# Split weights of the units with 256 moving columns, placed 64 bytes further on in their slots

## The reference, cut to what matters

```python
z = h @ w_in                              # odd: 1024 -> 3104 columns
proj = h @ w_in[l]                        # mix: 1024 -> 3584 columns
q = (h @ w_q).reshape(B, S, MEM_HEADS, MEM_HEAD_DIM)
k, v = jnp.split(m @ w_kv, 2, axis=-1)    # m: the 256 memory tokens
x = x + 0.5 * swiglu_2(rmsnorm(x, ffn2_norm[l]), ffn2_w_gu[l], ffn2_w_down[l])
```

## Time and profile before

| | us |
|---|---|
| three runs, median | 2511.64 |
| three runs, lowest and highest | 2505.56, 2512.35 |
| the profiled execution, its own time | 2508.56 |
| its span, first instruction to last | 2506.6 |
| PE busy | 2434.8 (97% of the span) |
| weight loads busy | 2029.8 (81%) |
| DVE, ACT, POOL busy | 1238.3, 892.2, 74.3 |
| granted TensorE clock, mean | 0.984 of full speed |

### The profile page before, as it was taken

How to read it: one execution, slowest core, us unless ns; L and a number is a source line. 1 busy time by engine, 2 the same in 40 slices (tenths; PEclk the granted TensorE clock), 3 DMA queues, 4 the chain that set the end, 5 groups by cost and what they waited for, 6 DMA issues and landing times.

```text
span 2506.6 us, 30267 instructions
## 1 busy us (share of the span) xinstructions
PE 2434.8 (97%) x12270; PEld 2029.8 (81%) x12270; DVE 1238.3 (49%) x1476; ACT 892.2 (36%) x1202; POOL 74.3 (3%) x81
## 2 busy tenths in 40 slices
PE   7989999999999999999999999999989999999998
PEld 6658888888899778888888888789968877888886
DVE  6687543357746543332354442446676544444423
ACT  3353323313345333332333331335355444333311
POOL 0210000000012000000000000000000000000000
PEclk9999999998999999999999999999999999999999
DMA  8215522463232222222222222221111212222221
GB/s 333 77 69 234 184 104 97 151 247 139 93 123 88 78 69 99 100 100 96 89 84 100 100 94 100 87 101 68 68 51 68 84 68 84 84 100 98 87 101 66
DMA packets 40405, 267.34 MB, mean 107 GB/s; under 512 B 4378, under 2 KB 5658, under 8 KB 9218
## 3 DMA queue, kind: packets, MB, share of 16 engines
q1 hardware_dynamic: 31248, 219.87, 24.4%
q0 software_dynamic: 5696, 40.37, 4.2%
q10 hardware_dynamic: 3378, 5.91, 0.8%
HBM read 263.90 MB, written 2.24 MB: 106 GB/s over the span
## 4 chain that ended last, share of the span: by engine, by line
PE 88%; DVE 7%; ACT 3%; DMA 1%; issue 1%; SPq 0%; DVEq 0%; ACTq 0%
PE bank L227 26%; PE bank L228 25%; PE bank L229 25%; PE bank L2223 1%; DVE w_lo L214 1%; ACT w_hi L210 1%; DMA work<-stream 1%; PE bank L2138 1%; PE bank L330 1%; PE bank L1864 1%; PE bank L2200 1%; DVE work L457 1%; PE bank L2212 1%; DVE work L441 1%; PE bank L1860 1%
## 5 line engine op out<-in xcount | busy, mean ns | idle before, releaser
L227 PE MATMUL bank<-h_hi,w_hi 128*128 128x512 f32 x1800 | 711.6, 395 | 5.4 <-DVE w_lo L214 2.2
L228 PE MATMUL bank<-h_lo,w_hi 128*128 128x512 f32 x1800 | 704.0, 391 | 0.0
L229 PE MATMUL bank<-h_hi,w_lo 128*128 128x512 f32 x1800 | 703.8, 391 | 0.0
L214 DVE TENSOR_TENSOR w_lo<-raw,w_hi 128x2048 fp32r<-128x2048 f32 x192 | 439.9, 2291 | 478.9 <-ACT w_hi L210 478.9
L210 ACT ACTIVATE w_hi<-raw 128x2048 fp32r<-128x2048 f32 x192 | 366.3, 1908 | 414.0 <-PE bank L229 410.5
L227 PEld LDWEIGHTS bank<-h_hi,w_hi 128*128 128x128 f32 x1800 | 340.0, 189 | 82.6 <-issue 6.7
L229 PEld LDWEIGHTS bank<-h_hi,w_lo 128*128 128x128 f32 x1800 | 339.9, 189 | 71.8
L228 PEld LDWEIGHTS bank<-h_lo,w_hi 128*128 128x128 f32 x1800 | 340.1, 189 | 70.5 <-issue 1.4
L229 PE MATMUL bank<-g_hi,w_lo 128*128 (+1 forms) x704 | 273.9, 389 | 0.0
L227 PE MATMUL bank<-g_hi,w_hi 128*128 (+1 forms) x704 | 273.9, 389 | 0.0
L228 PE MATMUL bank<-g_lo,w_hi 128*128 (+1 forms) x704 | 273.9, 389 | 0.0
(11 more groups left out here) (321 smaller groups left out, 2799.7 us busy)
## 6 DMA issues: line engine op xcount, KB each, us to landing
raw<-stream SPq DMA_DIRECT2D x192, 1024.0 KB, 4.8
work<-stream POOLq DMA_DIRECT2D x19, 1024.0 KB, 7.0
h_plain<-stream POOLq DMA_DIRECT2D x16, 1024.0 KB, 5.4
work<-stream SPq DMA_DIRECT2D x13, 1024.0 KB, 12.3
work<-mlstm_rows ACTq DMA_DIRECT2D x8, 512.0 KB, 4.8
x<-xT SPq DMA_DIRECT2D x1, 2048.0 KB, 9.8
outT<-work SPq DMA_DIRECT2D x8, 256.0 KB, 2.2
work<-mlstm_rows ACTq DMA_DIRECT2D x8, 192.0 KB
```

The source lines that it names most:

```text
L214: nc.vector.tensor_tensor(w_lo[:, slot(m), :], raw[:, slot(m), :], w_hi[:, slot(m), :], ALU.subtract).then_inc(lo_split, 1)
L227: nc.tensor.matmul(out, stationary[0], moving[0], start=first, stop=False)
L228: nc.tensor.matmul(out, stationary[0], moving[1], start=False, stop=False)
L229: return nc.tensor.matmul(out, stationary[1], moving[0], start=False, stop=last)
```

## The change

Each of the two slots of `w_hi` and `w_lo` grows by 32 words (128 bytes). A set `beside` lists the 22 units with 256 moving columns, and a helper `words(m)` gives the place of unit m within its slot: from word 16 (64 bytes) for those, from word 0 for all others. Both splits write there, and all readers take it from there. No instruction is added, removed or moved on any engine, and `raw` stays as it was.

Addresses after: `w_hi` 82048 as before and its second slot 128 bytes further on than before; `w_lo` 98688, that is 256 bytes further on, its second slot 384; everything behind them 512 bytes further on (`work` 125824). All these steps are multiples of 128. So, counted modulo 128, only the weights of the 22 units move, by 64.

```diff
--- before.py
+++ after.py
@@ -113,8 +113,8 @@
         h_lo = place("h_lo", [P, KC, S], F32R)
         h_plain = place("h_plain", [P, 4, UNIT], offset=at[0] - 4 * UNIT * 4)
         raw = place("raw", [P, 2, UNIT])
-        w_hi = place("w_hi", [P, 2, UNIT], F32R)
-        w_lo = place("w_lo", [P, 2, UNIT], F32R)
+        w_hi = place("w_hi", [P, 2, UNIT + 32], F32R)
+        w_lo = place("w_lo", [P, 2, UNIT + 32], F32R)
 
         par = place("par", [P, N_PARAMS])
         tab = place("tab", [P, N_TABLES])
@@ -198,6 +198,15 @@
         def slot(m):
             return m % 2
 
+        beside = set()
+        for name, units in (("odd_in", range(5, 13)), ("mix_in", (4, 5, 6, 7, 12, 13)), ("mem_kv", range(7)), ("mem", (4,))):
+            beside.update(FIRST_UNIT[name] + u for u in units)
+
+        def words(m):
+
+            c = 16 if m in beside else 0
+            return slice(c, c + UNIT)
+
         def place_of(m):
 
             return ADA_UNITS + m
@@ -207,11 +216,11 @@
             act.wait_ge(landed[slot(m)], 16 * (m // 2 + 1) + 16 * i)
             if m >= 2:
                 act.wait_ge(unit_used, m - 1 + 2 * i)
-            nc.scalar.activation(w_hi[:, slot(m), :], raw[:, slot(m), :], ACT.Copy).then_inc(hi_split, 1)
+            nc.scalar.activation(w_hi[:, slot(m), words(m)], raw[:, slot(m), :], ACT.Copy).then_inc(hi_split, 1)
 
         def split_lo(dve, m, i=0):
             dve.wait_ge(hi_split, m + 1 + 2 * i)
-            nc.vector.tensor_tensor(w_lo[:, slot(m), :], raw[:, slot(m), :], w_hi[:, slot(m), :],
+            nc.vector.tensor_tensor(w_lo[:, slot(m), words(m)], raw[:, slot(m), :], w_hi[:, slot(m), words(m)],
                                     ALU.subtract).then_inc(lo_split, 1)
 
         def split_next_hi(act, m, i=0):
@@ -230,7 +239,7 @@
 
         def unit_cols(m):
 
-            return [w[:, slot(m), :].rearrange("p (k n) -> p k n", k=KC) for w in (w_hi, w_lo)]
+            return [w[:, slot(m), words(m)].rearrange("p (k n) -> p k n", k=KC) for w in (w_hi, w_lo)]
 
         def features(pe, m, block, out, wait_chunk=None, src=None, i=0):
 
@@ -834,7 +843,7 @@
 
                 def rows(d, i, first=False, end=False):
                     m = self.md + d
-                    wh, wl = (w[:, slot(m), :].rearrange("p (k n) -> p k n", k=2) for w in (w_hi, w_lo))
+                    wh, wl = (w[:, slot(m), words(m)].rearrange("p (k n) -> p k n", k=2) for w in (w_hi, w_lo))
                     pe.wait_ge(lo_split, m + 1 + 2 * i)
                     order = [(k, o) for k in range(2) for o in range(KC)]
                     early, late = 2 * slot(self.md), 2 * slot(self.md + 1)
```

## The result

The changed kernel is slower: 2526.25 us (median of 4 runs, 2524.55 to 2530.14) against 2510.54 for the kernel before beside it (2505.56 to 2512.35). The ratio is 1.0073, 95% interval 1.006 to 1.0086. The prediction, 2506.5 with a range up to 2520, is missed on the slow side. The profiled execution took 2525.41 us with a span of 2523.4; before, 2508.56 with 2506.6. So 16.8 us have to be found in the trace, at the same mean granted clock (0.984 in both).

A forecast was written before the change was run, and what follows sets the result against it. TensorE was taken as the bound, paced by intervals between matmul starts. From the profiled 2508.6 us, 2.6 us gained on 256-column matmuls, all else 0, gave 2506.0; allowing for run scatter it predicted 2506.5, range 2495 to 2520.

The forecast's parts named there:

- TensorE is the bound, and what a matmul gains or loses arrives at the end: Whole kernel: TensorE busy 97% of the span; a matmul's gain or loss where the changed units run arrives almost one to one.
- The addresses decide: Weight load beside matmul stream: their phase, and so addresses, sets the interval; 256 columns settle at a poor value, 120 ns.
- the restart rows: Profile rows after a break: eight 256-column intervals average 117.5 ns against 120 settled; ten 512-column ones 231 against 226.8.
- Rival A: Placement plays no part; the 13 ns are a fixed price of a float32r matmul with its load: 2508.6 us, chance 0.12.
- 256 columns at 118 ns, 2.6 us gained: The 22 changed units: 1300 settled intervals go from 120 to 118 ns, gaining 2.6 us.
- Rival B: 256-column matmuls: load and stream no longer meet, interval 111.6 to 115 ns, gain 7.5 to 12.9 us, chance 0.34.
- C: 256-column matmuls: load and stream meet more often, 4.2 to 13 ns each, 6.8 to 21 us lost, chance 0.15.
- Modulo 128 a shift by 64 is the same either way, so one answer serves all 1728.: The 22 units' 1728 matmuls: shifting load or stream by 64 bytes was taken to have one and the same effect.
- Splits at nothing: 22 of the 192 ACT and DVE splits, 64 bytes further on: covered by PE, taken as 0; 4.6 us if uncovered.
- A step of 256 does not matter then; one of 128 no row shows. I take 0.: Second slots 128 bytes further on, `w_lo` 256, `work` 512: effect of these moves on everything else taken as 0.
- Rival D: Second slots' 128 bytes matter for every other unit of all shapes: half of 5400 at 3 ns, 8 us, 2517, chance 0.04.
- The signs to look for: Trace checks: about 256 instructions in the 30 us 256-column run, 134 in the 512-column window, loads 0.19 us, splits unchanged.

## Why the prediction was wrong

- *TensorE is the bound, and what a matmul gains or loses arrives at the end.* Right: +16.2 us busy, +16.8 us of span.
- *The addresses decide.* Right, as the restart rows had suggested. Moving only the activations (ratio 1.0112) shows it without the change. Rival A falls. That load and stream collide is the reading that fits; no run shows the collision itself.
- *256 columns at 118 ns, 2.6 us gained.* The sign held; the size was half. In the changed kernel the long run settles at 117.8 in one slot and 113.3 in the other, and all gain 3.1 ns in the mean, 5.1 us. The kernel with the shift and 256 bytes of room has 117.8 in the long run, the value forecast. That it was hit is partly luck: it came from the average of restarted intervals, and the same argument would have given 118 for 192 bytes, which settled at 113.3. Rival B was right for some units and C for none.
- *"Modulo 128 a shift by 64 is the same either way, so one answer serves all 1728."* The runs do not bear this out: the period is 256 and the sign counts. With 64 bytes and a room of 256 the weights that move settle at 117.8, and the units of `mem_kv` with weights that stay run at 113.5 in their longest stretch, in the mean at 115.7 to 116.1.
- *Splits at nothing.* Right: 1908 and 2290 ns.
- *"A step of 256 does not matter then; one of 128 no row shows. I take 0."* This is the step that failed, and the forecast with it. The first half holds (the room of 256 bytes). The second gave the value 0 and the chance 0.04 to a term for which no bounds were taken, though it touched half of all units and so some 4000 of the 512-column matmuls, more than twice as many as the change names. Bounds from both sides by the nearest rows were worked out for 1728 matmuls and not for these. By the earlier trace rows the term would have had an upper bound of 4.2 to 13 ns each, 17 to 52 us for 4000; a range that ends at 2520 holds not even the lower.
- *Rival D's price, 3 ns on half of 5400, 8 us.* The mechanism was right, and both factors too small: 5.5 ns on 3981 matmuls (`g`, `o` and `mixed` streams count as well), 21.8 us. Less the 5.1 gained, plus 0.8 in the first slots, that is the loss. D's own text had the direction ("512 columns sit near their best phase"), and what stood against it was a step of 256 alone, which says nothing of 128.
- *The signs to look for.* The loads kept their 0.19 us. 133 in the 512-column window was named as D's, and came. The 256 instructions in the 256-column run came too, but stand for a mean of two paces. The odd pieces and the long run moved the same way. The interval was not to leave 115 to 125; the mean of 116.5 stays inside, the second slots of the long run with 113.3 do not.

The Trainium skill, "SBUF — State Buffer", section "SBUF: two separate sides", says that TensorE's two read ports are independent and never wait on anyone, and the prediction drew from it that nothing would change. The runs contradict that: with `h` alone moved by 128 bytes against the weights, a 512-column matmul takes 232.6 ns rather than 226.7. The gap of "TensorE: Matmul & The Clock Gate", section "Back-to-back issue gap", 109.2 ns for 256 columns by its formula, was reached in no settled unit; the lowest is 113.3. In the Trainium skill that formula stands for the isolated gap, not for a stream of loads and matmuls, so it was no measure of what 64 bytes could free.

**What stays open.** What the two reads collide on was not measured, only that the addresses and the previous state decide. Why one distance settles at 113.3 once and at 117.8 another time is open as well. The unit with both paces shows that it can change across a dip of the clock; what then selects the pace was not tried, and with one trace of each kernel it is not known whether it is the same in every execution. Nor is it explained why 128 bytes give 232.4 ns where only the second slots have them and 233.2 where all units of a stretch do.

## What to carry to other kernels

Padding a double-buffered tensor moves its second slot and all that lies behind it: count the instructions whose operands move, not those that the change names, and give an unmeasured distance its full bounds times that count. In a kernel of this kind, bound at the full clock by float32r matmuls that each load their weights, compare the byte addresses of stationary and moving operands modulo 256 for every pair; here 512 columns wanted 0 or 16, and 256 columns a place such as 64 or 192. Pad by 256 bytes and measure a few shifts, since the best gain here was 0.3% and the wrong 128 bytes cost 0.7 to 1.1%.

## What was not expected of the hardware

- The interval of a float32r matmul depends on where its stationary operand begins against its moving one, in bytes: at 512 columns 226.7 to 226.9 ns at 0 and 16, 228.5 to 234.2 at the other places tried. 256 bytes are as none, 128 are not.
- A single word matters: 4 bytes off, 232.3 ns; 16 bytes off, 226.9.
- The state passes from one matmul to the next: with only `w_lo` displaced, a third of the matmuls, the mean is 230.9 to 233.1, and all three kinds of matmul are slower.
- The sign of the distance counts at 256 columns: with weights that stay, 64 bytes give 113.5 ns in the stretch shown and 192 give 117.5; with weights that move, 64 give 117.8 in the long run and 192 as little as 113.3.
- The same addresses have two settled paces at 256 columns, 113.3 and 117.8 ns, and a dip of the granted clock can lie between them.
